# Scaling attention outputs in transposed form and reordering the expert routing in a hybrid decoder block

## The reference, cut to what matters

```python
# attention (8 heads of 64): the 128 best keys of each query, chosen by an indexer
logits = einsum('bqhd,bqkhd->bhqk', q, k_sel) * 64 ** -0.5 - slopes * dist
p = softmax(logits); y = einsum('bhqk,bqkhd->bqhd', p, v_sel) @ w_attn_proj
mix = (g_ssm * y_ssm + g_att * y_att) @ w_o
h = layer_norm(ALPHA * h + mix)
# experts: top 4 of 32 by the router, softmax over the 4, tokens grouped by expert
logits = h @ w_router + b_router
top_val, top_idx = top_k(logits, 4); gates = softmax(top_val)
ffn = sum over the 4 of gate * (swiglu(h @ w_up[e] + b_up[e]) @ w_down[e] + b_down[e])
h = layer_norm(ALPHA * h + ffn)
```

## Time and profile before

| | |
|---|---|
| median of 3 runs | 1758.97 us (1758.9 to 1761.51) |
| the profiled execution | 1764.82 us |
| its span, first to last instruction | 1763.1 us |
| TensorE clock over the span | 0.973 of full speed |
| attention, from the last gate tile to the first projection tile | about 350 to 458 us |
| output projection and routing, to the first up product | about 488 to 569 us |
| loop over expert blocks begins | 609 us |

### The profile page before, as it was taken

The page is one execution under the profiler, slowest core; times in us unless marked ns, Lnnn a source line. Parts: engine busy times, 40 slices in busy tenths (PEclk is TensorE's granted clock), DMA queues, the critical chain, the costliest instruction groups (busy, mean ns, idle before and its releaser), DMA issues.

```text
span 1763.1 us, 22201 instructions
## 1 busy us (share of the span) xinstructions
PE 1686.9 (96%) x7129; PEld 1107.8 (63%) x7129; DVE 1499.1 (85%) x1710; ACT 1063.4 (60%) x1016; POOL 467.5 (27%) x298
## 2 busy tenths in 40 slices
PE   5899999999997999999999999999999999999996
PEld 2333344476576577777777777777777777777763
DVE  5999877555568799999999999999999999999995
ACT  4332222365445477777777777777777777777771
POOL 4855000064334111223121212222222212121210
PEclk9999899998998899999999999999999999999998
DMA  5111122110316789999999999999999999999973
GB/s 172 48 51 48 48 76 92 58 48 39 120 45 227 304 308 369 368 366 366 368 382 358 368 365 378 361 365 360 373 365 369 364 371 374 363 355 373 382 293 104
DMA packets 91901, 464.76 MB, mean 264 GB/s; under 512 B 21289, under 2 KB 21405, under 8 KB 42616
## 3 DMA queue, kind: packets, MB, share of 16 engines
q1 hardware_dynamic: 80240, 441.67, 65.9%
q0 software_dynamic: 9776, 18.41, 4.3%
q10 hardware_dynamic: 1848, 4.24, 0.7%
HBM read 454.15 MB, written 18.53 MB: 268 GB/s over the span
## 4 chain that ended last, share of the span: by engine, by line
PE 87%; DVE 9%; ACT 2%; issue 1%; DMA 0%; ACTq 0%; DVEq 0%
PE ps L1715 20%; PE ps L1717 20%; PE ps L1716 20%; PE ps L1515 6%; PE ps L1701 3%; PE ps L1442 2%; PE ps L1437 2%; PE ps L1723 2%; PE ps L1423 2%; PE ps L1431 1%; PE ps L1623 1%; PE ps L1622 1%; PE ps L1621 1%; PE ps L1576 1%; PE ps L1433 1%
## 5 line engine op out<-in xcount | busy, mean ns | idle before, releaser
L1163 DVE TENSOR_TENSOR w_lo<-raw,w_hi 128x2048 fp32r<-128x2048 f32 x384 | 874.1, 2287 | 76.3 <-ACT w_hi L832 76.2
L832 ACT ACTIVATE w_hi<-raw 128x2048 fp32r<-128x2048 f32 x384 | 737.0, 1920 | 244.6 <-PE ps L1717 244.2
L1715 PE MATMUL ps<-w_hi,x_hi 128*96 128x512 f32 x1024 | 415.9, 406 | 0.0
L1717 PE MATMUL ps<-w_lo,x_hi 128*96 128x512 f32 x1024 | 404.7, 395 | 0.0
L1716 PE MATMUL ps<-w_hi,x_lo 128*96 128x512 f32 x1024 | 404.4, 395 | 0.0
L1715 PEld LDWEIGHTS ps<-w_hi,x_hi 128*96 128x96 f32 x1024 | 169.3, 165 | 67.5 <-issue 1.5
L1717 PEld LDWEIGHTS ps<-w_lo,x_hi 128*96 128x96 f32 x1024 | 166.7, 163 | 71.1 <-issue 0.2
L1715 PE MATMUL ps<-w_hi,a_hi 128*96 128x512 f32 x512 | 204.6, 400 | 5.7 <-DVE a_lo L1261 5.7
L1716 PEld LDWEIGHTS ps<-w_hi,x_lo 128*96 128x96 f32 x1024 | 167.0, 163 | 64.0 <-issue 0.2
L1716 PE MATMUL ps<-w_hi,a_lo 128*96 128x512 f32 x512 | 201.8, 394 | 0.0
L604 POOL DMA_INDIRECT gate_now<-gate_rows,row_now x32 | 79.8, 2495 | 458.8 <-DVE tok_out L1291 443.7
(11 more groups left out here) (323 smaller groups left out, 2034.6 us busy)
## 6 DMA issues: line engine op xcount, KB each, us to landing
raw<-in_w_up SPq DMA_DIRECT2D x256, 1024.0 KB, 8.0
raw<-in_w_down SPq DMA_DIRECT2D x128, 1024.0 KB, 9.4
ring<-in_w_in SPq DMA_DIRECT2D x9, 2048.0 KB, 7.8
ring<-in_w_glu SPq DMA_DIRECT2D x4, 1024.0 KB, 6.3
ring<-in_w_o SPq DMA_DIRECT2D x2, 2048.0 KB, 11.7
h<-in_x SPq DMA_DIRECT2D x4, 512.0 KB, 4.9
ring<-in_w_attn_proj SPq DMA_DIRECT2D x1, 2048.0 KB, 8.9
h_rows<-h ACTq DMA_DIRECT2D x4, 512.0 KB, 3.6
```

Of the source, the lines that this page charges most:

```text
L832: s.activation(hi_of(c)[:, :], raw_of(c), ACT.Copy).then_inc(s_hi, 1)
L1163: d.tensor_tensor(lo_of(c)[:, :], raw_of(c), hi_of(c)[:, :], ALU.subtract).then_inc(s_lo, 1)
L1715: mm(o, xh, hi_of(c)[:, col], start=start, stop=False)
L1717: return mm(o, xh, lo_of(c)[:, col], start=False, stop=stop)
```

## The change

The transposed value products are made directly: the values (64 columns of a head) are the stationary operand and the transposed probabilities move, so bank 2 holds the output with channels on the rows; two heads go side by side to the two halves of the rows (`pv_pair`). The inverse row sums are spread over each head's 64 columns, transposed by TensorE (`inverse_T`) into bank 3, copied by ScalarE (`keep_inverse`), and VectorE multiplies bank 2 by them straight into `qiT` (`scaled_oT`). Probabilities get three buffers and their transposes four; TensorE's transposes run two steps behind the scores instead of one, and the unit's tile moves to odd i. ScalarE copies the transposes ahead of the next exponential, except at every fourth step. In the routing, norm1(3) goes ahead of choose(2), the marks are separated from the addresses, the addresses of tiles 1 and 2 are made in one go and those of tile 3 after the lower half of x; TensorE's and ScalarE's orders follow. The first up part no longer waits for the gates' transpose and the addresses; VectorE's wait for the list goes behind lo(-1, 7).

```diff
-        logit, prob, pT, glu_t = scr[:, 4:6], scr[:, 6:8], scr[:, 8:10], scr[:, 10:12]
-        oq, mix_t = scr[:, 12:13], scr[:, 13:16]
+        logit, glu_t, prob, pT = scr[:, 4:6], scr[:, 6:8], scr[:, 8:11], scr[:, 12:16]
+        inv_row, inv_T = scr[:, 11, :], part_lo
...
+            def keep_inverse(t):
+                act.wait_ge(s_invp, t + 1)
+                if t > 0:
+                    act.wait_ge(s_oT, t)
+                s.activation(inv_T[:, :], ps[3][:, :], ACT.Copy).then_inc(s_invT, 1)
 
             for i in range(len(STEPS) + 2):
+                if i >= 2 and i % 4 != 1:
+                    keep_pT(i - 2)
                 if i < len(STEPS):
                     exps(i)
-                if 1 <= i <= len(STEPS):
-                    keep_pT(i - 1)
-                if i % 4 == 3 and n < first_tile["at"]:
+                if i >= 2 and i % 4 == 1:
+                    keep_pT(i - 2)
+                if i % 4 == 2 and n < first_tile["at"]:
                     take(n)
                     n += 2
-                if i >= 2 and STEPS[i - 2][1] == HEADS - 1:
...
+                if i > HEADS and i % HEADS == 1:
+                    keep_inverse(i // HEADS - 1)
...
+            std(2)
...
+            rows_off(2)
+            keep_hT1(2)
+            std(3)
+            gate_exps(2)
+            rows_off(3)
+            keep_hT1(3)
+            hi(-1, 4)
+            gate_exps(3)
+            hi(-1, 5)
...
+            def inverse(t):
+                dve.wait_ge(s_pr, HEADS * t + HEADS)
+                step(d.reciprocal(rinv[:, :], rsum[:, t, :]))
+                if t > 0:
+                    dve.wait_ge(s_invp, t)
+                d.tensor_copy(inv_row.rearrange("p (h e) -> p h e", h=HEADS),
+                              rinv[:, :].unsqueeze(2).to_broadcast([P, HEADS, HD])).then_inc(s_inv, 1)
+
+            def scaled_oT(t):
+                dve.wait_ge(s_pv, HEADS // 2 * (t + 1))
+                dve.wait_ge(s_invT, t + 1)
+                d.tensor_tensor(qiT[:, :, P * t:P * t + P], ps[2][:, :].rearrange("p (k q) -> p k q", k=4),
+                                inv_T[:, :].rearrange("p (k q) -> p k q", k=4), ALU.mult).then_inc(s_oT, 1)
...
+            norm1(0)
+            choose(0)
+            norm1(1)
+            first_marks(0)
+            first_addresses(0, 1)
+            choose(1)
+            norm1(2)
+            norm1(3)
+            first_marks(1)
+            choose(2)
+            first_marks(2)
+            first_addresses(1, TT - 1)
+            choose(3)
+            first_marks(3)
+            lo(-1, 4)
...
+            first_addresses(TT - 1, TT)
             lo(-1, 5)
...
-            dve.wait_ge(s_slots, 16)
-            next_token(1)
             for c in range(7, 15):
                 lo(-1, c)
                 if c == 7:
+                    dve.wait_ge(s_slots, 16)
+                    next_token(1)
...
+            def pv_pair(i):
                 t, hh = STEPS[i]
-                pe.wait_ge(s_pT, i + 1)
+                pe.wait_ge(s_pT, i + 2)
                 if hh == 0 and t > 0:
-                    pe.wait_ge(s_on, t)
+                    pe.wait_ge(s_oT, t)
                 for c in range(t + 1):
-                    ins = mm(ps[2][:, HD * hh:HD * hh + HD], pT[:, i % 2, P * c:P * c + P],
-                             v[:, c, HD * hh:HD * hh + HD], start=c == 0, stop=c == t)
+                    for j in (i, i + 1):
+                        rows = slice(HD * (j % 2), HD * (j % 2) + HD)
+                        ins = mm(ps[2][rows, P * (hh // 2):P * (hh // 2) + P],
+                                 v[:, c, HD * (hh + j - i):HD * (hh + j - i) + HD],
+                                 pT[:, j % 4, P * c:P * c + P], start=c == 0, stop=c == t)
                 ins.then_inc(s_pv, 1)
...
-                if i % 2 == 0 and i > 0 and n < first_tile["at"]:
+                if i % 2 == 1 and n < first_tile["at"]:
                     tile(n, 9 + (n - first_tile["gg"]) // 8)
                     n += 1
-                if 1 <= i <= len(STEPS):
-                    probsT(i - 1)
-                if 2 <= i <= len(STEPS) + 1:
-                    pv(i - 2)
-                if i >= 3 and STEPS[i - 3][1] == HEADS - 1:
-                    o_T(STEPS[i - 3][0])
+                if 2 <= i < len(STEPS) + 2:
+                    probsT(i - 2)
+                if i > HEADS and i % HEADS == 1:
+                    inverse_T(i // HEADS - 1)
+                if i >= 4 and i % 2 == 0:
+                    pv_pair(i - 4)
...
-            place(TT - 2)
...
             first_rows(0)
+            route_T(TT - 1)
+            place(TT - 2)
+            route_lg(TT - 1)
             first_rows(1)
-            route(TT - 1)
             first_rows(2)
             place(TT - 1)
             first_rows(3)
...
-            pe.wait_ge(s_adr, TT)
-            pe.wait_ge(s_gdTe, 1)
             for p in range(8):
                 up_part(-1, p + 4, p)
                 if p == 1:
+                    pe.wait_ge(s_gdTe, 1)
                     pe.wait_ge(s_bias, 64)
```

More of the change, by code:

```diff
@@ L282, in build @@
         s_pTp, s_pT, s_pv = sem("probs_transposed"), sem("pT_ready"), sem("pv_done")
[L283 removed]
+        s_inv, s_invp, s_invT, s_oT = (sem(x) for x in ("inverse_rows", "inverse_transposed", "inverse_kept", "oT_ready"))
         s_mix = sem("mix_ready")
@@ L839, in _, with std, rows_off, keep_hT1 @@
             s.activation(brem, bias3[:, :], ACT.Copy).then_inc(s_bc, 1)
-            for t in range(TT):
+            def std(t):
                 act.wait_ge(s_var, TT + t + 1)
                 s.activation(rsx[:, t, 0:1], mvx[:, t, 1:2], ACT.Sqrt, bias=eps[:, 0:1]).then_inc(s_rstd, 1)
[L843 to L849, removed]
-                    s.activation(bias3[third, :], braw_b[third, :], ACT.Copy).then_inc(s_b3l, 1)
-                if t == 3:
-                    for c in range(4, 6):
-                        hi(-1, c)
+            def rows_off(t):
                 act.wait_ge(s_h1, t + 1)
                 act.dma_start(h1_rows.rearrange("(t p) d -> p t d", p=P)[:, t, :], h[:, t, :]).then_inc(s_h1row, 16)
+            def keep_hT1(t):
                 for r in range(2):
@@ L865, in _ @@
                              accum_out=gsum[:, 0:1]).then_inc(s_ge, 1)
+            std(0)
+            rows_off(0)
+            keep_hT1(0)
+            gate_exps(0)
+            std(1)
+            act.wait_ge(s_bs, 1)
+            step(s.activation(bias3[third, :], braw_b[third, :], ACT.Copy))
+            s.activation(brem[third, :], bias3[third, :], ACT.Copy).then_inc(s_bc, 1)
+            rows_off(1)
+            keep_hT1(1)
+            gate_exps(1)
+            std(2)
+            step(s.activation(bias3[second, :], braw_b[second, :], ACT.Copy))
+            act.wait_ge(s_bs, 2)
+            s.activation(bias3[third, :], braw_b[third, :], ACT.Copy).then_inc(s_b3l, 1)
+            rows_off(2)
[7 more added lines that the diff above has]
+            hi(-1, 5)
             def T_hi(dst, half, job, bank):
@@ L1112, in value @@
                 step(d.tensor_tensor(gate[:, i, :], gate[:, i, :], glu_t[:, i % 2, :], ALU.mult))
-            for i in range(len(STEPS) + 2):
+            for i in range(len(STEPS) + 4):
                 if i < len(STEPS):
                     logits(i)
+                if i > 0 and i % HEADS == 0:
+                    inverse(i // HEADS - 1)
                 if i % 4 == 1 and i > 1:
                     value(i // 4 - 1)
-                if i >= 2 and STEPS[i - 2][1] == HEADS - 1:
-                    t = STEPS[i - 2][0]
-                    dve.wait_ge(s_pv, i - 1)
-                    dve.wait_ge(s_pr, i - 1)
-                    step(d.reciprocal(rinv[:, :], rsum[:, t, :]))
-                    if t > 0:
-                        dve.wait_ge(s_oTp, t)
-                    d.tensor_tensor(oq.rearrange("p o (h e) -> p (o h) e", h=HEADS),
-                                    ps[2][:, :].rearrange("p (h e) -> p h e", h=HEADS),
-                                    rinv[:, :].unsqueeze(2).to_broadcast([P, HEADS, HD]), ALU.mult).then_inc(s_on, 1)
-                    dve.wait_ge(s_on, t + 1)
+                if i > HEADS and i % HEADS == 3:
+                    scaled_oT(i // HEADS - 1)
             def mix_lower(i):
@@ L1166, in _, with norm1 @@
             dve.wait_ge(s_gb2, 32)
-            for t in range(TT):
+            def norm1(t):
                 for r in range(2):
@@ L1182, in _, with choose @@
                     .then_inc(s_h1, 1)
-                if t > 0:
-                    first_addresses(t - 1)
-                if t == TT - 1:
-                    lo(-1, 4)
+            def choose(t):
                 dve.wait_ge(s_lgt, t + 1)
```

66 lines of the change are left out of this document (35 added, 31 removed).

## The result

The changed kernel takes 1738.78 us, the median of four runs (1736.2 to 1740.57), the kernel before 1760.24 (1758.9 to 1761.58). The ratio is 0.9875, 95% interval 0.9857 to 0.9893: 22 us less, where 30 was forecast. The profiled execution took 1740.57, its span is 1738.5.

What follows compares the result with a forecast made beforehand. TensorE, busy 96% of the span, was taken as the bound. Attention and projection 23.6 us plus routing 7.3 sum to 30.9, taken as 30, giving 1729 from a median of 1759; own range 1723 to 1735, eight in ten 1720 to 1744.

Steps and rivals of the forecast that it cites:

- (a): Rival for the attention's value products: the two column halves do not overlap, giving 1738; chance 0.12.
- (b): Rival: the clock stays low because switches and short transposes leave TensorE ragged, giving 1738.5; chance 0.15.
- The clock, 8.5 in the attention: Attention: with TensorE's idles gone, the falls to the lower clock level behind them go too, saving 8.5 us.
- forecast 1.0: Projection tiles: 1.0 of the 3.5 us lost to the low clock comes back, since one gap remains.
- forecast 6.0: Attention's value products by pairs on two column halves: 18.0 us becomes 12.0, including 0.20 per pair for switching; 6.0 saved.
- stalls' 5.25: Attention: TensorE's idles at the three changes of query tile, 5.25 us in all, go.
- the order of copies, 3.5: Attention: transposes two steps behind no longer wait for ScalarE's copies, mean 0.22 over 16 pairs, 3.5 us saved.
- The routing, 7.3: Routing up to the first up product: marks 5.5 us sooner and the gates' wait moved, 1.8 more; 7.3 us gained.
- the wait for place(3): Routing: the wait for place(3), now behind two sets of first rows on TensorE, was counted as 0.8 us.
- the 5.5: Routing: with norm1(3) ahead of choose(2), the marks of tile 3 come at 556.5 instead of 562.05, 5.5 us sooner.
- (c): Rival: list, slots and gather come late, TensorE gives the routing's 7.3 back at the gathered rows' transposes, 1736; chance 0.13.
- (d): Rival for the attention: ScalarE's copies become the bound as each pair's transposes wait for them, slower at 1776; chance 0.04.

Runs made afterwards that it cites:

- experiment 1: The attention's edits alone on the kernel before, routing unchanged: 1740.87 us, ratio 0.9889 to the kernel before.
- experiment 2: The routing's edits alone on the kernel before, attention unchanged: 1756.4 us, ratio 0.9966 to the kernel before.
- experiment 3: The changed kernel with first_rows(1) moved ahead of place(2) on TensorE: 1739.1 us, ratio 0.9863 to the kernel before.
- experiment 4: The changed kernel with TensorE made to wait for VectorE's scaled tile at each change of query tile: 1752.82 us, ratio 0.9943 to the kernel before.
- experiment 12: The kernel before, unedited, run and profiled once more: 1759.79 us, span 1757.7.
- experiment 9: The changed kernel with TensorE's wait for the gates' copy put back ahead of its first up part: 1741.13 us, ratio 0.988 to the kernel before.
- experiment 8: The changed kernel with value products issued ahead of the transposes in each step: 1733.67 us, ratio 0.9855 to the kernel before.
- experiment 5: Experiment 3 with tile 3's list addresses made directly behind its marks: 1738.25 us, ratio 0.9871 to the kernel before.
- experiment 10: Experiment 5 with VectorE's wait for the slots moved behind the ninth part's split and first row sums: 1735.58 us, ratio 0.9858 to the kernel before.
- experiment 7: The changed kernel with a pair's value products issued head by head instead of interleaved: 1743.46 us, ratio 0.9884 to the kernel before.
- experiment 11: Experiments 8 and 10 together: 1732.73 us, ratio 0.9838 to the kernel before.

## Why the prediction was right, and where it was off

The time lies in the range of 1720 to 1744, outside the forecast's own 1723 to 1735, and the order of the parts is as forecast: the attention earns most. The gain was forecast 9 us too high. The time is also the one that the forecast gave its rivals (a) and (b), 1738; what rules them out are the traces, not the time. Of the signs named ahead, the windows at full clock and 16 value instructions in about 1.1 us came; waits at transposes of at most 0.5 us (0.75 and 0.95) and the first up product near 538 (546.65) did not.

How much of the gain is clock can be estimated from all runs, since each has its span L and clock c on record. The mean of the forecast's (1-c)L, and what is left of the span, good to about 1 us since c has three digits:

| kernel | runs | (1-c)L | rest |
|---|---|---|---|
| before, on the chip of experiments 1 to 4 | 17 | 44.4 | 1715.7 |
| before, on the two other chips | 9 and 9 | 45.0 and 40.8 | 1715.2 and 1717.6 |
| after | 4 | 32.1 | 1704.5 |
| attention's edits alone | 5 | 34.1 | 1705.9 |
| routing's edits alone | 12 | 37.4 | 1717.0 |
| stall put back | 6 | 38.5 | 1712.3 |

The change took 9 to 13 us of clock, over the whole kernel, where 9.5 were forecast, and 11 to 13 us of all else, where 21.4 were forecast (14.15 in the attention, 7.3 in the routing). So the forecast was too high in what it counted at full clock, and its clock term came out near right as a sum.

*The clock, 8.5 in the attention: an amount read from one execution.* The same instructions with the same idles took 108.5 us at 0.92, 100.7 at 1.00 (experiment 12) and 105.4 at 0.95 (experiment 2): 7.8, 0 and 4.7 lost, 4.2 in the mean. (The forecast's (1-c)L is a little high besides, since an idle at the low level loses nothing.) Eleven traces have the new attention; eight show 1.00. Two (experiments 3 and 9) show 0.98 and 91.0 us: behind TensorE's idle of 1.9 for the first GLU tile, which all have, they have 3 us at 0.50. The eleventh is experiment 4, with idles of 2.8 at the changes. So without the long idles at the changes no fall follows them, as argued, but what they cost before differs from run to run. The projection is alike: forecast 1.0, and 3.0, 1.7 and 0 by the three traces of the old code (30.2, 28.9 and 27.2 against 27.2), 1.6 in the mean. That the clock's sum is near the forecast's 9.5 is in part luck: these two places give 5.8 of it by the traces, and the rest lies where none was forecast, as in the first parts.

*The attention at full clock, 14.15 forecast (5.25 + 1.4 + 3.5 + 6.0 - 2.0): 10.9 measured*, 100.7 to 89.8. Experiment 12's window has TensorE busy for 89.43 and idle for 11.27; after it is 83.96 and 5.83. So the instructions' own time fell by 5.5, forecast 6.0. The products themselves went from 18.0 to 11.2 (0.37, 0.59, 0.81 and 1.02 a pair by query tile, four pairs of each), better than the 12.0 of the forecast, since in and out cost 0.15 there instead of 0.20; 1.3 less than that shows in the busy time, and which of the instructions around them take it was not measured. One change of division per pair need not be, as experiment 8 shows, at 0.17 us each. The Trainium skill (TensorEngine Tiling, Tiling Modes) says that each change of mode drains TensorE; experiment 8 agrees in kind. The idles fell by 5.4, forecast 8.15. Of the stalls' 5.25, 1.03 is left (0.28 and 0.75). What was mis-sized is the order of copies, 3.5: I took the lag between products and transposes as idle, but the waits for copies outside the three changes were 7.2 - 5.25 = 2.0 by the earlier trace rows. And the new waits are 2.8, the 1.03 among them, where 2.0 was left for them. Part of that is the spreading copy, which the forecast priced at 0.70 and as costing nothing: it took up to 1.98, and the wait of 0.75 is behind it. At the end 0.85 is left, where 1.0 was forecast.

*The routing, 7.3: this is the step that failed.* The prediction's sum has VectorE's selection of tile 3 out 13.5 us behind place(1) (its 556.5 for the marks less the 0.8, and less the 0.75 that pass before from chosen_b to the marks); it was 14.8, with 1.10 of wait for the router's products. Then the prediction counted the wait for place(3), "which now follows two sets of first rows on TensorE, as 0.8". It was 6.0, from 535.55, where chosen_b of tile 3 is out, to 541.55: 4.2 until place(3) starts behind the two sets, which take 7.02 us, and 1.8 until VectorE reads it. About 3 of the 7.02 are the lower level of the clock, by the 1.92 and 2.00 of a set in experiment 3; the forecast had no clock term in this stretch, which went from 0.82 to 0.73. So the marks came no sooner (21.0 us behind place(1), 20.6 before), and the 5.5 was zero. The gates' wait gave what was forecast: the first up product 1.8 sooner; in experiment 9 it comes 1.9 later behind x_lo, and 1.4 are left at the end.

Experiment 3 mends the failed step, with the first up product another 5 us sooner, and shows that it would have been worth nothing here: list and slots are late then, rival (c)'s mechanism, on VectorE instead of at the gathered rows. The slack of the list that the prediction counted (10 us shrinking to 3) was the gather's; that VectorE itself waits for the slots, ahead of splits that TensorE needs, was not in it. With the list written sooner (experiment 5) VectorE still waits as long for the slots, and with the wait behind other work (experiment 10) it does not: the stretch goes 64.6, 61.7, 59.1. By time none of the three is clear of after.

The terms as the traces give them: 10.9 for the attention at full clock, 4.2 and 1.6 for the two clock terms, and 2.8 for the stretch of the routing, 19.5 in all. The 2.8 is again a mean: 67.8, 68.4 and 64.8 with the old order (before, experiments 12 and 1), 63.4, 66.0, 65.4, 63.2 and 63.2 with the new (after, experiments 2, 4, 7 and 8). The ratio gives 22, with an interval from 19 to 25. The traces are few, so that 19.5 lies in it proves little.

Of the rivals, (a) falls by experiment 7 and (b) by the windows. (d) shows in small: waits for ScalarE's copies come to 2.8, 0.95 at most. (c) is near in what the routing gains, but the gain was lost at place(3) and not where (c) had it. What stays open is why the falls come in one execution and not in another, and why the routing's edits alone measured 6.0: by the table of all runs they took 7.0 of clock and nothing of the rest, in an attention and first parts whose falls differ between the traces, and where these 7.0 lie was not shown.

## What to carry to other kernels

A stretch's clock in one profile is a sample: before pricing falls behind idles as a gain, profile the unchanged kernel twice, and keep its range in the forecast; the spans and clocks of all runs then tell whether a gain is clock or not. When an instruction is moved behind others on an engine, its wait is the sum of what now stands ahead of it, each at the clock of that stretch, not a hop. And before counting a routing chain that ends sooner, find the next engine's waits behind it: here VectorE's wait for a DMA stood ahead of work that was ready, and with that wait in place moving TensorE's work (experiment 3) kept nothing of the 5 us.

## What the runs showed of the hardware

TensorE's granted clock is not set by the instructions and idles that the trace shows: idles of 1.54 to 1.97 us at the same three places went with 0.92 over the attention in one execution and 1.00 in another. Idles of up to 2.8 us at the changes gave 0.93 (experiment 4, one trace).

Column halves that are not interleaved still overlap: sixteen instructions take 1.58 us head by head and 1.09 interleaved (1.51 and 1.02 from start to next start), where sixteen of half the moving size one after the other took 1.80 before.

Two changes of division that follow directly on each other are cheaper than with whole-array work between: the attention takes 86.6 instead of 89.8 us, in the traces of experiments 8 and 11 alike.

VectorE's copy that spreads eight values over 512 columns depends on what GpSimd does. Of the four in the trace after, two ran while GpSimd was idle and took 0.43 us. One ran beside GpSimd's split of a weight and took 1.32, one beside its multiply of h and took 1.98, and both ended 0.28 us behind GpSimd's instruction. The multiply of VectorE, priced at 0.70, is no measure for it. The slow copy held up TensorE by 0.75 us at 394.38, through the logits and ScalarE's exponential. GpSimd, VectorE, ScalarE:

```profile
389.30 2.41 POOL L560 TENSOR_TENSOR h<-h,gb 128x1024 f32<-128x1024 f32 x1
390.01 1.98 DVE L1138 COPY scr<-rinv 128x512 f32<-128x512 f32 x1
393.26 0.62 ACT L788 ACTIVATE scr<-scr,amax 128x384 f32<-128x384 f32 x1 [2.72 <-DVE amax L1130]
```
